# A decoder trunk on one core: TensorE's reports carried by drains instead of matmuls

## What is computed

```python
for l in range(DEPTH):
    n = rms_norm(h, attn_norm[l]);  proj = n @ w_in[l]                 # 1024 x 3592
    mixed = concatenate([y_gdn, y_sc, y_diff]);  h = h + mixed @ w_out[l]
    h = h + peer_ffn(rms_norm(h, ffn_norm[l]), ...)

def peer_ffn(x, w_q, sub_keys, u_tab, v_tab):
    q = x @ w_q;  scores = einsum(q, sub_keys);  best = top_k(top_k + top_k, 16)   # 8 heads x 16
    hid = gelu(einsum('td,thkd->thk', x, u_tab[idx]))      # 128 rows of 1024 per token from in_peer_u
    return einsum('thk,thkd->td', gates * hid, v_tab[idx]) # and 128 rows from in_peer_v
```

## Time and profile before

| what | value |
|---|---|
| three executions: median, lowest, highest | 3606.18, 3597.86, 3606.44 us |
| profiled execution, first to last instruction | 3680.9 us |
| PE busy with 9038 matmuls; with 9038 weight loads | 2077.6 us (56%); 972.8 us (26%) |
| DVE busy; POOL busy; ACT busy | 2235.5 us (61%); 2002.9 us (54%); 829.9 us (23%) |
| mean granted clock of PE | 0.742 of full speed |
| DMA: moved, mean rate | 1247.14 MB, 339 GB/s |

### The profile page before, as it was taken

The page is one execution under the profiler, slowest core; times in us unless marked ns, Lnnn a source line. Parts: engine busy times, 40 slices in busy tenths (PEclk is TensorE's granted clock), DMA queues, the critical chain, the costliest instruction groups (busy, mean ns, idle before and its releaser), DMA issues.

```text
span 3680.9 us, 29623 instructions
## 1 busy us (share of the span) xinstructions
PE 2077.6 (56%) x9038; PEld 972.8 (26%) x9038; DVE 2235.5 (61%) x5009; ACT 829.9 (23%) x2489; POOL 2002.9 (54%) x2084
## 2 busy tenths in 40 slices
PE   7774575576754475496563446387564356632325
PEld 3532421233312232244221322143331132200001
DVE  3369767475578666845458666837558655558340
ACT  3212313132123122123222121213212212220211
POOL 1024555465557565636457655635646665666665
PEclk9787776787867687798776768688786677755656
DMA  8289799898999899979899879979989889999999
GB/s 258 84 304 361 266 376 334 300 409 318 361 346 358 332 366 386 387 293 366 335 375 359 325 288 406 370 278 372 337 341 357 328 323 349 376 367 372 376 369 344
DMA packets 345853, 1247.14 MB, mean 339 GB/s; under 512 B 39539, under 2 KB 39609, under 8 KB 344417
## 3 DMA queue, kind: packets, MB, share of 16 engines
q0 software_dynamic: 295744, 1075.38, 77.5%
q1 hardware_dynamic: 48656, 160.79, 12.0%
q10 hardware_dynamic: 1296, 9.08, 0.6%
HBM read 1238.90 MB, written 6.20 MB: 338 GB/s over the span
## 4 chain that ended last, share of the span: by engine, by line
DVE 23%; PE 22%; another core or an unknown queue 19%; issue 16%; POOL 9%; DMA 8%; ACT 4%; SPq 0%; DVEq 0%; POOLq 0%; ACTq 0%
PE work L869 10%; DVE ring L1166 9%; POOL ring L483 9%; PE work L839 5%; PE accs L853 4%; DMA ring<-in_peer_u,idxU 3%; PE work L830 2%; DMA ring<-in_peer_v,idxR 2%; DMA wring<-in_w_out 1%; DVE proj L1178 1%; DMA wring<-in_peer_wq 1%; DVE proj L1174 1%; DVE arena L1222 1%; DMA wring<-in_w_in 1%
## 5 line engine op out<-in xcount | busy, mean ns | idle before, releaser
L483 POOL DMA_INDIRECT ring<-in_peer_u,idxU x1024 | 994.0, 971 | 892.6 <-issue 278.9
L1166 DVE CUSTOM_DVE_ANT_0 ring<-ring,n2U 128x1024 f32<-128x1024 f32 x1024 | 1205.0, 1218 | 338.5 <-DMA ring<-in_peer_u,idxU 247.1
L483 POOL DMA_INDIRECT ring<-in_peer_v,idxR x1024 | 992.8, 970 | 743.0 <-issue 276.6
L853 PE MATMUL accs<-ring,wv 128*32 128x512 f32 x4096 | 720.8, 839 | 719.5 <-DMA ring<-in_peer_v,idxR 499.8
L869 PE MATMUL work<-wring,nT 128*128 128x449 f32 (+1 forms) x1152 | 564.3, 626 | 251.9 <-issue 86.8
L853 PEld LDWEIGHTS accs<-ring,wv 128*32 128x32 f32 x4096 | 148.7, 137 | 1206.3 <-issue 1118.5
L869 PEld LDWEIGHTS work<-wring,nT 128*128 128x128 f32 x1152 | 233.6, 210 | 547.8 <-issue 366.5
L547 ACT ACTIVATE wv<-stack,coefR 128x32 f32<-128x32 f32 x1024 | 235.4, 309 | 356.5 <-remote 178.1
L519 ACT ACTIVATE arena<-work 128x512 f32<-128x512 f32 (+3 forms) x208 | 113.2, 563 | 604.7 <-remote 296.1
L869 PE MATMUL work<-wring,n2A 128*128 128x449 f32 x384 | 167.1, 558 | 0.0
L519 ACT ACTIVATE proj<-work 128x512 f32<-128x512 f32 (+1 forms) x88 | 48.9, 577 | 489.0 <-PE work L869 221.6
(11 more groups left out here) (292 smaller groups left out, 2135.5 us busy)
## 6 DMA issues: line engine op xcount, KB each, us to landing
wring<-in_w_in SPq DMA_DIRECT2D x160, 449.0 KB
wring<-in_w_out SPq DMA_DIRECT2D x64, 512.0 KB
wring<-in_peer_wq SPq DMA_DIRECT2D x64, 512.0 KB
ring<-in_peer_u,idxU POOLq DMA_INDIRECT x1024
ring<-in_peer_v,idxR POOLq DMA_INDIRECT x1024
held<-in_peer_wq SPq DMA_DIRECT2D x16, 512.0 KB, 7.2
arena<-keys_scr ACTq DMA_DIRECT2D x8, 1024.0 KB
keys_scr<-ring SPq DMA_DIRECT2D x2, 1024.0 KB, 4.9
```

What stands on the lines that cost most here:

```text
L483: nc.gpsimd.indirect_dma_start(ring[:, s * D:(s + 1) * D], None, table, bass.IndirectOffsetOnAxis(ap=idx, axis=0)).then_inc(row_in[s], 16)
L853: ins = nc.tensor.matmul(acc[c][quarter(r), :], wv[:, d * QUARTER:(d + 1) * QUARTER], ring[:, s * D + 512 * c:s * D + 512 * c + 512], star ...
L1166: V.tensor_tensor_reduce(out=rw, in0=rw, in1=n2U[:], scale=1.0, scalar=0.0, op0=ALU.mult, op1=ALU.add, accum_out=hid[:, kk:kk + 1]).then_i ...
```

## The change

Every report of PE to another engine is taken off the matmul that carried it. In its place stands a drain of PE behind that matmul, and the drain raises the same semaphore by the same amount. This concerns the 256 reports of V units, the 352 of weight pieces and the 620 of filled banks, 1228 in all. The matmuls, their order, the banks, the waits and the table `PLAN` are the same: no instruction changes its place against another on any engine. The setup's own reports (bias strips, keys, conv taps) stay on their matmuls.

```diff
-            def filled(name, ins):
-                ins.then_inc(full[BANK[name][0]], 1)
+            def filled(name):
+                pe.drain().then_inc(full[BANK[name][0]], 1)
 ...
             def flip(name, blocks, cols=P):
                 w = fill(name)
                 for i, s in enumerate(blocks):
                     ins = nc.tensor.transpose(w[:, i * P:(i + 1) * P], s, ident[:])
-                filled(name, ins)
+                filled(name)
 ...
             def rows_v(k, q, row):
 ...
-                ins.then_inc(usedV, 1)
+                pe.drain().then_inc(usedV, 1)
 
             def product(kind, g, who, left, n):
 ...
                                 if kc == KC - 1 and name != names[-1]:
-                                    filled(name, ins)
-                    ins.then_inc(w_used, 1)
+                                    filled(name)
+                    pe.drain().then_inc(w_used, 1)
 ...
-                        filled(name, nc.tensor.matmul(w[:, 0:wide], qTa[o:o + 32, b * P:(b + 1) * P], keyT[o:o + 32, b * SEQ:b * SEQ + wide], start=True, stop=True))
+                        nc.tensor.matmul(w[:, 0:wide], qTa[o:o + 32, b * P:(b + 1) * P], keyT[o:o + 32, b * SEQ:b * SEQ + wide], start=True, stop=True)
+                        filled(name)
```

More of the change, by code:

```diff
@@ L909, in stage_a @@
                 nc.tensor.matmul(w[:, 0:4], triu[:], g, start=True, stop=True)
-                filled(f"gcum.{k}", nc.tensor.matmul(w[:, 4:8], ones[:], g, start=True, stop=True))
+                nc.tensor.matmul(w[:, 4:8], ones[:], g, start=True, stop=True)
+                filled(f"gcum.{k}")
                 pe.wait_ge(S["g_ready"], nth("g_ready", k, 2))
@@ L959, in stage_a @@
                     ins = nc.tensor.matmul(w[:, s], nwT[:, s], state[:, s], start=False, stop=True)
-                filled(f"vn.{k}", ins)
+                filled(f"vn.{k}")
                 mix("vn")
@@ L968, in stage_a @@
                     ins = nc.tensor.matmul(w[:, s], et[:, s], vnew[:, s], start=False, stop=True)
-                filled(f"oo.{k}", ins)
+                filled(f"oo.{k}")
                 heads(f"sn.{k}", [(kn[:, h * P:(h + 1) * P], vnew[:, h * P:(h + 1) * P]) for h in range(GH)])
@@ L993, in values @@
                                                vcache[:, kt * 256 + 64 * h:kt * 256 + 64 * h + 64], start=(kt == 0), stop=(kt == wide // P - 1))
-                    filled(f"pv{h}.{k}", ins)
+                    filled(f"pv{h}.{k}")
                 logits(0)
```

## The result

The kernel after takes 3887.47 us (median of 4, from 3868.96 to 3890.31). Beside it the kernel before took 3602.02 us (4 executions, 3592.52 to 3606.44). The ratio is 1.0803, with a 95% interval of 1.0759 to 1.0846: 285 us slower. The forecast was 3702 us, its range ended at 3840. The sign was right and the size three times too small: 96 us were forecast.

What follows compares the result with a forecast made beforehand. No engine owned the chain; transfers were near their limit. 818 drains at 0.33 us, 0.39 on the path, gave 105 us, plus 11 for reports; 0.83 kept made 96, added to 3606: 3702 us, range 3545 to 3840.

Steps and rivals of the forecast that it cites:

- The price of a drain: Between overlapping PE matmuls: 0.33 us per drain, from 0.16 lost overlap, 0.11 weight load, 0.06 sequencer; bounds 0.16 to 0.60.
- The count: Of PE's 1228 reports, at least 818 have the next matmul right behind, where a drain takes something away.
- The report's own delay: At the 410 reports with a gap behind, a drain reports 0.07 us later: 11 us, between 0 and 29.
- One mark for it: Sign expected in the profile after: PE's gaps number over 1000 instead of 410.
- the share on the path, 0.39: PE is on the path for 810 us of 2077.6 busy, so 0.39 of added PE time counts: 270 us become 105.
- the 0.83 kept: Stretches set by POOL (9%) and DMA (8%) gathers hide a slower PE, so 96 of 116 us are kept.
- The chain's "unknown" 19% and "issue" 16%: Shares of the chain that ended last, listed as another core or an unknown queue, and issue, beside PE's 22%.
- rival A: Faster: drains' reports pass PE's late matmul reports, winning at most 227 us of idle DMA: 3475 us, half 3589; chance 0.22.
- the bounds of the forecast case: The forecast case's own range, 3640 to 3810 us, from 51 and 191 + 29 us less what transfers cover; chance 0.59.
- Rival B: Slower still: drains stand behind late completions, 35 pieces at 10.6 instead of 1.72 us, 121 us on top: 3823 us; chance 0.08.
- The clock term of B: An emptier PE spends a tenth of the products' 864 us at a lower clock: 34 us more.
- Rival C: No change: PE waits 410 times anyway and drains shorten later waits; under 11 us, 3606 to 3617 us; chance 0.11.

Runs made afterwards that it cites:

- half_after: The kernel after with gathers of 512 columns instead of 1024: 3211.79 us with reports on time, 3849.56 us where they are late.
- half_before: The kernel before with gathers of 512 columns instead of 1024: 3031.91 us with reports on time, 3547.49 us where they are late.
- after_third: The kernel after, unchanged, run once more where reports were on time: 3328.48 us, 1.0292 times the kernel before.
- bare_again: The kernel before plus a drain that reports nothing behind each of the 1228 reporting matmuls, repeated with reports on time: 3320.20 us, ratio 1.0252.
- bare drains: The kernel before plus a non-reporting drain behind each of the 1228 reporting matmuls, run where reports were late: 3934.77 us, ratio 1.0807.
- v_only: The kernel before with only the 256 V unit reports moved to drains, reports on time: 3240.83 us, ratio 1.0020.

## Why the prediction was wrong

**The price of a drain held.** 0.33 us was forecast, 0.34 measured (2.06 against 1.72 us per piece). It holds beyond the pieces: matched matmul by matmul, half_after against half_before has 761 reports with the next matmul right behind and equal lengths around them, and they cost 265 us of PE time, 0.35 each (four transposes 0.30, the groups of eight in the ladder 0.32 to 0.49). A second drain adds 0.08. The Trainium skill (TensorE: Matmul & The Clock Gate, "Step-by-step: what each phase is for") says that a matmul's way out of the array overlaps the next one's way in. The rows agree in kind: pieces of 1.88 us by their modelled ends start 1.72 us apart in the earlier trace rows, and behind a drain they don't overlap. Which share of the 0.34 is this overlap no run shows. The count held too: some 830 reports of the kernel before have the next matmul within 0.15 us, where 818 were taken. The report's own delay was forecast at 11 us and measured at 8 (after_third less bare_again), within the scatter.

**One mark for it was badly chosen.** Over 1000 gaps were forecast, and there are 774. Pieces 0.08 us apart by their modelled ends (1.98 long, 2.06 from start to start) are not listed as gaps. The interval between starts was the mark that told.

**The step that failed is the share on the path, 0.39, together with the 0.83 kept.** Together with 11 us for the reports they gave 96 us for 270 us of PE time. With most of the cover gone and reports on time the change costs 180 (share 0.67); in the batches like the one forecast, 285 to 302, more than the whole 270. Three errors are in it:

- A mean share over PE's busy time was used, while drains lie unevenly. Where reports are late, 256 V drains cost 17 us (0.07 each), 620 bank drains 176 (0.28), 352 piece drains 138 (0.39, more than the full price). V units are off the path, products and ladder on it. The earlier trace rows gave L853 4% of the span, 0.2 of its 721 us busy; L869 10%, 0.43 of its 864; L839 5%, 0.7 of its 263. So that V counts least could have been read; that a piece costs more than a bank could not.
- The chain's "unknown" 19% and "issue" 16% were left out of PE's share. With them it is 22 + 19 + 16 = 57%, 2098 us for 2078 busy: a share of one. The late reports were PE's, as rival A itself argued, so behind them stood PE's work. This is read after the fact, and not all of the two shares need be PE's; no run isolates it.
- The cover was counted where it hardly was. 96 us is nearly what the change costs on time, 94, but that is a coincidence: there DMA is at 1.01 and, by the difference of the two pairs, hides half of the 180. At 0.93, in the earlier trace rows, that cover is thin: with half rows the cost is 302, beside 285 and 292, no more than the scatter.

Smaller faults of the working: all pieces of the earlier trace rows carry a report, so they don't show that groups with and without one have the same pitch; the 10.6 us between two releases in the earlier trace rows hold nearly all of the 7.31 us in which PE itself stood, so they are no measure of how late a report is; and the bounds of the forecast case, 51 and 220 us times 0.83, give 3648 to 3789, not 3640 to 3810. None of them carries the miss.

**Rival A fell, and its premise was half right.** The late reports did exist in the timed executions: the kernel's time differs by 11% with them. The Trainium skill (NOTIFIC — the notification-queue block, "Overflow: three behaviours, one of which stalls the engine") was the ground for doubting this. It has a rule by which records are dropped and one by which the block's inside pushes back instead of losing them; missing records, as below, would be the first and slowed completions the second, and no run here shows either at work. But a drain does not pass a late completion. DMA fell to 0.89 where A wanted over 0.95, and bare drains, which cannot make any report earlier, cost the same as the change (298 beside 285 and 292 us).

**Rival B's mechanism is in the trace, and was given 0.08.** Drains stand behind late completions: 241 of them, some 900 us. B had counted 35 pieces at 8.9 us more, 311 us, and no banks. What this adds to the price is by subtraction: 285 - 180 = 105 us, and 302 - 180 = 122 for the pair of half rows. These differences are between batches of two kinds, so the split of 285 into about 180 of lost overlap and 105 of standing is argued, not shown: the same 270 us with a larger share on the path would give the same times, and no run separates the two. By this split B's part is the smaller one. It would be one ninth of the 900 us that the drains stood; V's half of them is off the path, and why the other half counts so little is open. The clock term of B did not appear: 0.742 before, 0.750 after.

**Rival C** fell: no interval of the whole change reaches 1.00. For V drains alone on time its "under 11 us" does hold (+5 and +9 us).

**What stays open** is where the lateness comes from. It is not the amount of DMA traffic (0.67 was as late as 0.93), nor the chip as such (two of them showed both), nor the drains (before has it). Of the engines it is nearly PE alone. I matched each rise of a semaphore that the trace records with the nearest earlier end of an instruction that makes it, which can only make it look less late than it is. In before, 370 of 1097 matched matmul reports of PE come over 1 us late, 2182 us in all, against 9 of 684 of ACT and 42 of 1516 of DVE; in half_before only the very last of 1246 of PE comes over 0.06 us late. The clock explains little of the 366 us between 3602 and 3236: it is lower where reports are late, but PE's busy time differs by 61 us only (2077.6 in before, 2016.3 in v_only). The best lead is the record itself. The trace of every on-time profile holds 43,448 to 43,489 rises of semaphores; the late ones hold 18,915 to 22,664 for the same number of updates, half rows or not, drains or not. Nearly all that is missing is of other engines and queues: of the 22,804 rises that before lacks against v_only, 21,299 are landings of DMAs, while 1097 of PE's 1245 are there. In before, the first 200 us have 1788 rises, v_only has 1854, and no matched report of PE is over 1 us late there; from 400 us on before has some 700 to 1300 in 200 us where v_only has 2570 to 2860, and a fifth to seven tenths of PE's matched reports are late. Records go missing when PE's completions come late. That fits a recording path that is overrun and holds PE up, but it is a coincidence of two signs and not a test: every execution here has its span and clock listed, so none is known to have run without a record. Whether an execution without one would show 1.03 or 1.08 for this change is open. No version tried beats the kernel before.

## What to carry to other kernels

Leave a report on the matmul that makes the data. A drain between back-to-back matmuls of this kernel costs about a third of a microsecond of PE whether or not it carries the report, and when a completion is late it stops PE, which otherwise runs on. When costing added PE time, weigh it kind by kind by the lines of the chain, ask whose reports the chain's "unknown" and "issue" shares wait for (that they belong to PE here is a reading, not a test), and allow cover only where another engine or DMA is really at its limit. And compare only with the kernel before beside it: the same edit was worth 1.029 in one batch and 1.080 and 1.082 in two others.

## What the runs showed of the hardware

- One kernel, unchanged, took 3235 to 3238 us in some batches and 3592 to 3640 in others, 11 to 13% more, steady within each. The traces differ in late completions of PE's matmuls, and in the granted clock: 0.79 to 0.80 on time (v_only, after_third), 0.74 to 0.75 late, where PE stands more.
- All profiles with late completions lack about half of the semaphore records, and no other profile lacks any to speak of (20 profiles, one to one); in before, 21,299 of the 22,804 missing ones are landings of DMAs.
- A drain behind a piece at full clock costs PE 0.34 us and a second one at the same place 0.08 (starts 1.72, 2.06 and 2.14 us apart).
- A completion can be over 10 us behind its matmul's end while no other work runs on PE (the drain of 17.4 us around a piece of 5.3), and a drain waits for it.
- Half the gathered bytes gave 6.4% in one kind of batch and 1.2% in the other. An experiment that lightens the load of one resource says something only beside the kind of batch in which it ran.
